# The first eight modulation slabs: from a sum on VectorE to products on TensorE

## The chip, the cores and the metric

One core of a Trainium2 chip runs the kernel. The metric is the device time of one execution in microseconds (us). Before the change the median of 3 runs is 2600.26 us (2599.4 to 2601.9).

## The reference, cut to what matters

The model is two blocks in a row on 256 tokens of width 2048. The work around the change is the very beginning of the first block:

```python
cond = jax.nn.silu(c)                       # (1, 2048)
mod = cond @ ada_w[i] + ada_b[i]            # ada_w[i]: (2048, 6144)
shift, scale, gate = jnp.split(mod, 3, axis=-1)
h = rms_norm(x, pre_g[i]) * (1 + scale[:, None, :]) + shift[:, None, :]
y = sgu_mixer(h, sgu_w_in[j], ...)          # begins with h @ w_in, w_in: (2048, 12288)
```

Everything is float32. The large products are made from rounded parts: a value is split into a high part (float32r) and the rest, and three products (high by high, rest by high, high by rest) are added.

## The kernel before, in words

All weights stream from HBM through a ring `raw` of four slabs of 1 MB (`RAWS = 4`; a slab is four tiles of 128 rows by 512 columns). SyncE's queue issues the loads in the order in which they are used (`load`, L291). Before each it waits for `raw_free`, which starts at four and which VectorE raises by one each time it has finished with a slab (`raw_done`, L1022 to L1027). The landing of slab n is told by the semaphore `landed[n % 4]`.

The first eight slabs of the ring (`ADA_HEAD = 8`) belong to `ada_w[0]`: four for the first 512 columns (the shift of model columns 0 to 511) and four for columns 2048 to 2559 (the scale of the same model columns). After them come the slabs of `sgu_w_in`, mixed with further slabs of `ada_w[0]`.

How `cond @ ada_w` is made before: the weight tile has the contracted rows on the partitions. VectorE multiplies each 128x512 tile by one column of `cond` (one number for each partition) and adds it to a running sum, in two chains (`ada_sum`, L1037; L1051 is the first product of a chain, L1047 a product with addition, L1056 adds the two chains). A slab costs four such instructions. When four slabs are summed, TensorE adds over the partitions (`pe_ada`, L1946): four matmuls with 128 columns of the sum as the stationary operand and a column of ones as the moving one, so each has one moving column. VectorE copies the four resulting columns out of PSUM (`ada_keep`, L1060).

The start, engine by engine:

- ScalarE loads `x` by DMA, waits for the small vectors, makes `cond` by Silu (L613), squares the two tiles of `x` for the norm (L535), takes the root (L542), scales both tiles to `y` (L619), and copies the eight groups of turned tiles out of PSUM into `xt` (L622).
- TensorE turns the small vectors (L2068, L2069), then the two tiles of `y` in eight groups of four 128x128 transposes (L2077), two PSUM banks in turn, then makes the two column sums (L1952).
- VectorE makes the eight slabs' sums with the steps of the norm in between, and then the shift and scale of the first four column tiles (`modulated`, L1258 to L1260, which tells `scales`).
- Then ScalarE writes the modulated tiles `tf` (L631, four instructions, one for each column tile) and their rounded part `a_hi` (L558, two), VectorE the rest `a_lo` (L1268, two), and the first product with `w_in` begins on TensorE (`pe_block`, `pe_chunk`, L1927 and L1932).

From there the work is in four phases of twelve blocks. Each phase covers four of the sixteen contracted column tiles, each block two chunks. For each chunk ScalarE rounds half a slab (`hi_next`, L437) and VectorE makes the rest (`lo_next`, L1018), three chunks ahead of TensorE (`AHEAD = 3`). The eight other slabs of `ada_w[0]` in each phase are summed by VectorE in the same way as the first eight.

Of the kernel before, what the change touches and what calls it, by code (L numbers as in the profile page):

```python
# [22 lines left out]
P = 128  # L23
T = 2
# [139 lines left out]
def build(nc, d, out):  # L164
    ctx = ExitStack()
    with ctx:
# [3 lines left out]
        def sem(name):  # L170
            return ctx.enter_context(nc.semaphore(name))
# [109 lines left out]
        lb_diff, lb_exp, h_gn, h_kf = (sem(k) for k in ("lb_diff", "lb_exp", "h_gn", "h_kf"))  # L281
        wt_zero, h_a_zero = sem("wt_zero"), sem("h_a_zero")
        lb_ready = sem("lb_ready")

# [7 lines left out]
        def load(sp, n, *parts):  # L292

            k = n.raw.base % RAWS
            sp.wait_ge(raw_free, n.raw.at(1))
            for place, source, adds in parts:
                sp.dma_start(place(raw[:, k, :]), source).then_inc(landed[k], adds)
            n.raw.base += 1
# [309 lines left out]
        def _(act):  # L608
            n = Counts()
            for t in range(T):  # L610
                act.dma_start(x[:, t, :], d["x"][0, t * P:(t + 1) * P, :]).then_inc(x_landed, 16)
            act.wait_ge(vec_kept, 1)
            nc.scalar.activation(cond[:, :], va[:, A_C:A_C + KT], ACT.Silu).then_inc(cond_ready, 1)  # L613
            act.wait_ge(x_landed, 32)
            act_squares(act, n, lambda t: x[:, t, :])
            act_root(act, n)
            act.wait_ge(n_rstd, n.nrm.base)
            for t in range(T):
                nc.scalar.activation(y[:, t, :], x[:, t, :], ACT.Copy, scale=rstd[:, t:t + 1]).then_inc(n_out, 1)  # L619
            for g in range(8):  # L620
                act.wait_ge(t_turned, g + 1)
                nc.scalar.activation(xt[:, 2 * g:2 * g + 2, :], ps[:, 3 + g % 2, :].rearrange("p (k s) -> p k s", k=2), ACT.Copy).then_inc(xt_kept, 1)  # L622

            def modulated(p):

                act.wait_ge(scales, p + 1)
                if p:
                    act.wait_ge(t_lo, 2 * p)
                for g in range(2 * p, 2 * p + 2):
                    for k in range(2 * g, 2 * g + 2):  # L630
                        ins = nc.scalar.activation(tf[:, g % 2, k % 2 * S:(k % 2 + 1) * S], xt[:, k, :], ACT.Identity,  # L631
                                                   bias=mod[:, 0, k:k + 1], scale=hscale[:, k:k + 1])
                    ins.then_inc(t_kept, 1)
                act_split(act, n, 2, a_hi[:, 4 * p:4 * p + 4, :], modulated=True, fresh=True)

# [424 lines left out]
        def ada_keep(dve, n, layer, col, bank=7, at=0):  # L1060

            dve.wait_ge(ada_summed, n.ada.at(1))
            nc.vector.tensor_copy(mod[:, layer, bass.ds(col, 4)], ps[:, bank, at:at + 4]).then_inc(ada_kept, 1)
            n.ada.base += 1
# [167 lines left out]
        def _(dve):  # L1232
# [3 lines left out]
            nc.vector.tensor_copy(vb[:, :], ps[:, 4, P:P + B_ROWS]).then_inc(vec_kept, 1)  # L1236
            dve.wait_ge(cond_ready, 1)
            early = (ps[:, 6, :], ps[:, 5, :])
            ada_sum(dve, n, 0, acc, early)
            n.sq.base += 2  # L1240
            dve.wait_ge(n_ss, n.sq.base)
            nc.vector.tensor_scalar(var[:, :], ss[:, :], 1.0 / D, EPS, ALU.mult, ALU.add).then_inc(n_var, 1)
            ada_sum(dve, n, 1, acc, early)
            dve.wait_ge(n_sd, n.nrm.base + 1)
            nc.vector.reciprocal(rstd[:, :], sd[:, :]).then_inc(n_rstd, 1)
            n.nrm.base += 1
            ada_sum(dve, n, 2, acc, early)
            ada_sum(dve, n, 3, acc, early)
            for a in range(3):
                ada_sum(dve, n, a, acc_s, early)  # L1250
            ada_keep(dve, n, 0, 0)
            ada_sum(dve, n, 3, acc_s, early)

# [24 lines left out]
            def phase_sum(m):  # L1278

                j = m % PHASE_W  # L1280
                if m < FIRST and j < PHASE_A:
                    ada_sum(dve, n, j % 4, (acc, acc_s)[j // 4], early)

            lo_next(dve, n, 0)
            ada_keep(dve, n, 0, 16)
            modulated(0)
            split(0)
# [659 lines left out]
        def pe_ada(pe, n, acc=acc, bank=7, at=0):  # L1947

            pe.wait_ge(ada_acc, n.ada.at(1))
            pe.wait_ge(ada_kept, n.ada.at(1))  # L1950
# [112 lines left out]
        def _(pe):  # L2063
# [6 lines left out]
            pe.wait_ge(vec_kept, 2)  # L2070
            pe.wait_ge(n_out, 2)
            for g in range(8):
                if g >= 2:
                    pe.wait_ge(xt_kept, g - 1)
                for k in range(2 * g, 2 * g + 2):
                    for t in range(T):
                        ins = nc.tensor.transpose(ps[:, 3 + g % 2, k % 2 * S + t * P:k % 2 * S + (t + 1) * P], y[:, t, k * P:(k + 1) * P], ident)  # L2077
                ins.then_inc(t_turned, 1)
            pe_ada(pe, n)
            pe_ada(pe, n, acc_s)  # L2080
            pe.wait_ge(xt_kept, 8)
            for p in range(PHASES):
                n.tg.base += 2
                n.kept.base += 2
                pe.wait_ge(t_lo, n.tg.base)
                for j in range(PHASE_W):
                    pe_block(pe, n, A, kts=4, k0=4 * p)
                    if j in (3, 7):
# [413 lines left out]
```

## Time and profile before

| What | Value |
| --- | --- |
| median of 3 runs | 2600.26 us |
| the profiled execution | 2598.19 us |
| its span (first to last instruction) | 2596.4 us |
| TensorE matmul busy | 2523.9 us, 97% |
| VectorE busy | 1631.5 us, 63% |
| ScalarE busy | 1361.4 us, 52% |
| mean DMA rate | 211 GB/s |
| mean granted TensorE clock | 0.991 |

The profile is of one execution. In its rows PE is TensorE's matmuls, PEld its loads of the stationary operand (they run beside matmuls), DVE VectorE, ACT ScalarE, POOL GpSimd, SP SyncE; a `q` behind a name is the engine's queue of DMA issues. `L1047` is line 1047 of the kernel. `a <- b` names the tile written and those read. Times are in us from the span's start, unless a row says ns. In square brackets stands the idle time of the engine ahead of a row and what ended it. PEclk is the granted clock of TensorE as a share of full speed: 1.00 is 2.4 GHz, 0.50 is 1.2 GHz.

### The profile page before, as it was taken

The page shows a single profiled execution, that of the slowest core. Times are in us where ns is not written, and L with a number is a line of the kernel's source. Part 1 is how long each engine was busy: PE and PEld are TensorE (multiplying, and loading weights), DVE is VectorE, ACT ScalarE, POOL GpSimd, SP SyncE. Part 2 cuts the span into 40 slices and gives each one's busy share as a digit, 9 for nine tenths or more (in the row PEclk, how much of TensorE's full clock was granted, in tenths as well). Part 3 has the DMA queues.
Part 4 walks back from the last instruction along what each step waited for, and adds up shares of the span by engine and source line. Part 5 has one row for each costly group of instructions (what it writes and reads, how often), then busy time and mean ns, then how long its engine had stood idle before and what let it go on. Part 6 is the DMA issues. An engine that isn't in the chain of part 4 may idle for free.

```text
span 2596.4 us, 33485 instructions
## 1 busy us (share of the span) xinstructions
PE 2523.9 (97%) x11958; PEld 2086.4 (80%) x11958; DVE 1631.5 (63%) x2512; ACT 1361.4 (52%) x1922; POOL 412.6 (16%) x288
## 2 busy tenths in 40 slices
PE   4999999999997999998999999999999999999999
PEld 3788788888886888887887787888888888888887
DVE  7779987767666677766655554555555545545544
ACT  4555764444446555555466666654544444444443
POOL 0155563111020000010000000034100011110111
PEclk8999999999998999999999999999999999999999
DMA  9889877877773776654645555545555555555554
GB/s 347 319 272 345 297 248 259 276 279 274 253 278 130 225 213 199 208 175 135 193 147 176 157 159 155 172 169 182 191 191 183 194 193 181 194 194 179 182 191 146
DMA packets 363831, 549.06 MB, mean 211 GB/s; under 512 B 32332, under 2 KB 126128, under 8 KB 363312
## 3 DMA queue, kind: packets, MB, share of 16 engines
q1 hardware_dynamic: 361872, 541.24, 63.0%
q10 hardware_dynamic: 1824, 6.04, 0.6%
q8 instruction: 83, 1.36, 0.2%
q14 instruction: 52, 0.43, 0.0%
HBM read 545.13 MB, written 2.10 MB: 211 GB/s over the span
## 4 chain that ended last, share of the span: by engine, by line
PE 92%; DVE 3%; issue 3%; ACT 2%; DMA 0%; SPq 0%; POOL 0%; ACTq 0%; DVEq 0%; POOLq 0%
PE ps L1927 54%; PE ps L1932 27%; PE ps L1912 1%; PE ps L1914 1%; PE ps L1913 1%; DVE ps L1047 1%; PE ps L2003 1%; PE ps L2234 1%; PE ps L1952 1%; DVE lo L1018 1%; ACT hi L437 1%; PE ps L2107 1%; PE ps L2233 1%; ACT tf L597 0%; PE ps L1989 0%
## 5 line engine op out<-in xcount | busy, mean ns | idle before, releaser
L1018 DVE TENSOR_TENSOR lo<-raw,hi 128x1024 fp32r<-128x1024 f32 x838 | 1081.5, 1302 | 749.6 <-ACT hi L437 748.7
L437 ACT ACTIVATE hi<-raw 128x1024 fp32r<-128x1024 f32 x838 | 881.6, 1060 | 759.8 <-PE ps L1932 658.9
L1927 PE MATMUL ps<-hi,a_hi 128*128 128x512 f32 (+1 forms) x2144 | 852.0, 397 | 6.9 <-issue 4.7
L1927 PE MATMUL ps<-hi,a_lo 128*128 128x512 f32 (+1 forms) x2144 | 837.3, 391 | 0.0
L1932 PE MATMUL ps<-lo,a_hi 128*128 128x512 f32 (+1 forms) x2144 | 574.1, 390 | 0.4 <-DVE lo L1018 0.4
L1927 PEld LDWEIGHTS ps<-hi,a_hi 128*128 128x128 f32 x2144 | 404.0, 188 | 95.4 <-issue 11.6
L1932 PEld LDWEIGHTS ps<-lo,a_hi 128*128 128x128 f32 x2144 | 402.9, 188 | 85.5 <-DVE lo L1018 1.0
L1927 PEld LDWEIGHTS ps<-hi,a_lo 128*128 128x128 f32 x2144 | 404.0, 188 | 79.3
L1927 PE MATMUL ps<-hi,b_hi 128*128 128x512 f32 x1024 | 404.1, 395 | 0.3 <-ACT y L766 0.3
L1927 PE MATMUL ps<-hi,b_lo 128*128 128x512 f32 x1024 | 399.4, 390 | 0.0
L1932 PE MATMUL ps<-lo,b_hi 128*128 128x512 f32 x1024 | 274.3, 390 | 0.0
L1932 PEld LDWEIGHTS ps<-lo,b_hi 128*128 128x128 f32 x1024 | 192.2, 188 | 40.9
L1927 PEld LDWEIGHTS ps<-hi,b_hi 128*128 128x128 f32 x1024 | 192.4, 188 | 39.1 <-ACT y L766 0.5
L1927 PEld LDWEIGHTS ps<-hi,b_lo 128*128 128x128 f32 x1024 | 192.4, 188 | 38.7
L1787 POOL TENSOR_TENSOR v<-v,stage 128x512 f32<-128x512 f32 (+1 forms) x88 | 145.0, 1648 | 436.6 <-ACT stage L456 295.1
L1047 DVE SCALAR_TENSOR_TENSOR ps<-raw,cond,ps 128x512 f32<-128x512 f32 x200 | 141.3, 749 | 1.1 <-DMA raw<-in_ada_w 1.1
L456 ACT ACTIVATE stage<-ps 128x512 f32<-128x512 f32 x156 | 84.6, 595 | 90.4 <-PE ps L1932 90.4
L1787 POOL TENSOR_TENSOR x<-x,stage 128x512 f32 (+1 forms) x38 | 65.5, 1722 | 355.2 <-ACT stage L456 351.9
L1787 POOL TENSOR_TENSOR v<-stage 128x512 f32 x32 | 34.2, 1069 | 323.0 <-ACT stage L456 319.8
L1787 POOL TENSOR_TENSOR v<-v 128x512 f32<-128x512 f32 x16 | 29.0, 1834 | 330.3 <-ACT v L466 330.0
L1787 POOL TENSOR_TENSOR y<-y,stage 128x512 f32<-128x512 f32 x30 | 50.9, 1696 | 168.5 <-ACT stage L456 166.3
L1047 DVE SCALAR_TENSOR_TENSOR acc_b<-raw,cond,acc_b 128x512 f32<-128x512 f32 x84 | 66.9, 797 | 0.0
(289 smaller groups left out, 1912.0 us busy)
## 6 DMA issues: line engine op xcount, KB each, us to landing
raw<-in_ada_w SPq DMA_DIRECT2D x96, 1024.0 KB
raw<-in_sgu_w_in SPq DMA_DIRECT2D x96, 1024.0 KB
raw<-in_w_up SPq DMA_DIRECT2D x64, 1024.0 KB
raw<-in_w_down SPq DMA_DIRECT2D x64, 1024.0 KB
raw<-in_w_in SPq DMA_DIRECT2D x42, 1024.0 KB
raw<-in_sgu_w_out SPq DMA_DIRECT2D x32, 1024.0 KB
raw<-in_w_in SPq DMA_DIRECT2D x128, 256.0 KB
raw<-in_mla_w_in SPq DMA_DIRECT2D x33, 512.0 KB
```

The lines of the kernel that those rows point to most:

```text
L437: nc.scalar.activation(hi[:, q % CHUNKS, :], raw[:, r % RAWS, q % 2 * CW:(q % 2 + 1) * CW], ACT.Copy).then_inc(hi_ready, 1)
L456: nc.scalar.activation(to, ps[:, 2 * s + t, 0:width], func, scale=rstd[:, t:t + 1] if normed else 1.0).then_inc(acc_free, 1)
L1018: nc.vector.tensor_tensor(lo[:, q % CHUNKS, :], raw[:, r % RAWS, q % 2 * CW:(q % 2 + 1) * CW], hi[:, q % CHUNKS, :].bitcast(F32), ALU.subt ...
L1047: ins = nc.vector.scalar_tensor_tensor(out=out[:, :] if a == j == 3 else to, in0=w, scalar=c, in1=to, op0=ALU.mult, op1=ALU.add)
L1787: return nc.gpsimd.tensor_tensor(out_, a, b, op)
L1912: mm(out_, w_hi, x_hi, start=start, stop=False)
L1913: mm(out_, w_hi, x_lo, start=False, stop=False)
L1914: return mm(out_, w_lo, x_hi, start=False, stop=stop)
L1927: nc.tensor.matmul(ps[:, 2 * s + t, 0:width], x[:, k0 + j, t * P:(t + 1) * P], hi[:, c, w], start=begins, stop=False)
L1932: ins = nc.tensor.matmul(ps[:, 2 * s + t, 0:width], x2[0][:, k0 + j, t * P:(t + 1) * P], lo[:, c, w], start=False, stop=last and j == kts - 1)
L1952: ins = nc.tensor.matmul(ps[:, bank, at + q:at + q + 1], acc[:, q * P:(q + 1) * P], ones[:, :], start=True, stop=True)
L2003: ins = nc.tensor.transpose(ps[:, 4 + n.tg.base % 2, e2 * S + t * P:e2 * S + (t + 1) * P], src(t, 2 * g + e2), ident)
```

## The change

- TensorE now makes the first eight slabs' products itself. `slab_product(a)` waits for slab a and makes sixteen matmuls: each has a 128x128 piece of the slab as the stationary operand and one column of `cond` as the moving one. The sixteen pieces of the contraction are added in PSUM, banks 4 to 7. VectorE's eight `ada_sum` calls and TensorE's two `pe_ada` calls at the start go.
- The loads of ring slabs 4 to 11 wait for `slab_used`, which TensorE raises after each product, and not for `raw_free`. VectorE adds eight to `raw_free` at once when all products are done, for the loads after them.
- Products and transposes of `x` are interleaved in TensorE's order: slabs 0 and 1, three groups of transposes, slab 2, three groups, slab 3, two groups, slab 4, slabs 5, 6 and 7.
- ScalarE squares `x` before it waits for the small vectors and makes `cond` (before: after it).
- The second tile of `y` is scaled by VectorE, and every second group of turned tiles is copied by VectorE (`xt_vec`).
- One VectorE copy takes all eight columns (shift and scale) out of PSUM. It stands ahead of the first `lo_next`.
- Of the first four modulated column tiles, ScalarE makes two and VectorE two (`tf_vec`), and TensorE's first chunk of each phase waits only for the first of the two groups of `a_lo`; it waits for the second after that chunk.

```diff
         def load(sp, n, *parts):
             k = n.raw.base % RAWS
-            sp.wait_ge(raw_free, n.raw.at(1))
+            if n.raw.turn is None and RAWS <= n.raw.base < ADA_HEAD + RAWS:
+                sp.wait_ge(slab_used, n.raw.base - RAWS + 1)
+            else:
+                sp.wait_ge(raw_free, n.raw.at(1))
...
+            act.wait_ge(x_landed, 32)
+            act_squares(act, n, lambda t: x[:, t, :])
             act.wait_ge(vec_kept, 1)
             nc.scalar.activation(cond[:, :], va[:, A_C:A_C + KT], ACT.Silu).then_inc(cond_ready, 1)
-            act.wait_ge(x_landed, 32)
-            act_squares(act, n, lambda t: x[:, t, :])
             act_root(act, n)
             act.wait_ge(n_rstd, n.nrm.base)
-            for t in range(T):
-                nc.scalar.activation(y[:, t, :], x[:, t, :], ACT.Copy, scale=rstd[:, t:t + 1]).then_inc(n_out, 1)
-            for g in range(8):
+            nc.scalar.activation(y[:, 0, :], x[:, 0, :], ACT.Copy, scale=rstd[:, 0:1]).then_inc(n_out, 1)
+            for g in range(0, 8, 2):
                 act.wait_ge(t_turned, g + 1)
-                nc.scalar.activation(xt[:, 2 * g:2 * g + 2, :], ps[:, 3 + g % 2, :].rearrange("p (k s) -> p k s", k=2), ACT.Copy).then_inc(xt_kept, 1)
+                nc.scalar.activation(xt[:, 2 * g:2 * g + 2, :], ps[:, 0, :].rearrange("p (k s) -> p k s", k=2), ACT.Copy).then_inc(xt_kept, 1)
...
-                for g in range(2 * p, 2 * p + 2):
+                for g in range(2 * p, 2 * p + 2 if p else 1):
...
+                if p == 0:
+                    act_split(act, n, 1, a_hi[:, 0:2, :], modulated=True, fresh=True)
+                    act.wait_ge(tf_vec, 1)
+                    act_split(act, n, 1, a_hi[:, 2:4, :], modulated=True, fresh=True)
+                else:
+                    act_split(act, n, 2, a_hi[:, 4 * p:4 * p + 4, :], modulated=True, fresh=True)
...
-            dve.wait_ge(cond_ready, 1)
             early = (ps[:, 6, :], ps[:, 5, :])
-            ada_sum(dve, n, 0, acc, early)
...
-            ada_sum(dve, n, 1, acc, early)
...
-            ada_sum(dve, n, 2, acc, early)
-            ada_sum(dve, n, 3, acc, early)
-            for a in range(3):
-                ada_sum(dve, n, a, acc_s, early)
-            ada_keep(dve, n, 0, 0)
-            ada_sum(dve, n, 3, acc_s, early)
+            dve.wait_ge(n_rstd, n.nrm.base)
+            nc.vector.tensor_scalar(y[:, 1, :], x[:, 1, :], rstd[:, 1:2], None, ALU.mult).then_inc(n_out, 1)
+            for g in range(1, 8, 2):
+                dve.wait_ge(t_turned, g + 1)
+                nc.vector.tensor_copy(xt[:, 2 * g:2 * g + 2, :], ps[:, 1, :].rearrange("p (k s) -> p k s", k=2)).then_inc(xt_vec, 1)
+            dve.wait_ge(slab_used, ADA_HEAD)
+            nc.vector.tensor_copy(mod[:, 0, 0:32].rearrange("p (c k) -> p c k", c=2)[:, :, 0:4],
+                                  ps[:, 4:8, 0:2].rearrange("p q c -> p c q")).then_inc(ada_kept, 2)
+            n.ada.base += 2
+            nc.vector.memset(tick[:, 0:1], 0.0).then_inc(raw_free, ADA_HEAD)
+            n.raw.base += ADA_HEAD
...
+            modulated(0)
+            dve.wait_ge(scales, 1)
+            dve.wait_ge(xt_vec, 4)
+            for k in range(2, 4):
+                ins = nc.vector.tensor_scalar(tf[:, 1, k % 2 * S:(k % 2 + 1) * S], xt[:, k, :], hscale[:, k:k + 1], mod[:, 0, k:k + 1], ALU.mult, ALU.add)
+            ins.then_inc(tf_vec, 1)
             lo_next(dve, n, 0)
-            ada_keep(dve, n, 0, 16)
-            modulated(0)
             split(0)
...
             pe.wait_ge(vec_kept, 2)
-            pe.wait_ge(n_out, 2)
-            for g in range(8):
+            pe.wait_ge(cond_ready, 1)
+
+            def slab_product(a):
+                pe.wait_ge(landed[a % RAWS], LAND * (a // RAWS + 1))
+                for r in range(4):
+                    for q in range(4):
+                        k = 4 * (a % 4) + r
+                        ins = mm(ps[:, 4 + q, a // 4:a // 4 + 1], raw[:, a % RAWS, r * NB + q * P:r * NB + (q + 1) * P], cond[:, k:k + 1],
+                                 start=k == 0, stop=k == KT - 1)
+                ins.then_inc(slab_used, 1)
+
+            def x_turned(g):
                 if g >= 2:
-                    pe.wait_ge(xt_kept, g - 1)
+                    pe.wait_ge(xt_vec if g % 2 else xt_kept, g // 2)
                 for k in range(2 * g, 2 * g + 2):
                     for t in range(T):
-                        ins = nc.tensor.transpose(ps[:, 3 + g % 2, ...], y[:, t, k * P:(k + 1) * P], ident)
+                        ins = nc.tensor.transpose(ps[:, g % 2, ...], y[:, t, k * P:(k + 1) * P], ident)
                 ins.then_inc(t_turned, 1)
-            pe_ada(pe, n)
-            pe_ada(pe, n, acc_s)
-            pe.wait_ge(xt_kept, 8)
+
+            slab_product(0)
+            slab_product(1)
+            pe.wait_ge(n_out, 2)
+            for a, groups in ((2, (0, 1, 2)), (3, (3, 4, 5)), (4, (6, 7))):
+                for g in groups:
+                    x_turned(g)
+                slab_product(a)
+            for a in range(5, ADA_HEAD):
+                slab_product(a)
+            n.ada.base += 2
+            pe.wait_ge(xt_kept, 4)
+            pe.wait_ge(xt_vec, 4)
             for p in range(PHASES):
                 n.tg.base += 2
                 n.kept.base += 2
-                pe.wait_ge(t_lo, n.tg.base)
+                pe.wait_ge(t_lo, n.tg.base - 1)
                 for j in range(PHASE_W):
-                    pe_block(pe, n, A, kts=4, k0=4 * p)
+                    pe_block(pe, n, A, kts=4, k0=4 * p, extra=None if j else {0: lambda: pe.wait_ge(t_lo, n.tg.base)})
```

## Rows read from the trace of the kernel before

**Rows 1.** The page: busy time, and the chain that ended last by engine.

```profile
PE 2523.9 (97%) x11958; PEld 2086.4 (80%) x11958; DVE 1631.5 (63%) x2512; ACT 1361.4 (52%) x1922; POOL 412.6 (16%) x288
...
PE 92%; DVE 3%; issue 3%; ACT 2%; DMA 0%; SPq 0%; POOL 0%; ACTq 0%; DVEq 0%; POOLq 0%
```

**Rows 2.** Stretches: window, us, busy of each engine, PEclk, DMA share, GB/s.

```profile
core 0: us, PE busy (x) PEld busy (x) DVE busy (x) ACT busy (x) POOL busy (x), PEclk, DMA share, GB/s
...
27.90:31.30 3.40, 2.56 (x21) 2.17 (x20) 3.40 (x8) 2.18 (x4) 0.00 (x0) 1.00 1.05 404
31.40:43.40 12.00, 1.86 (x8) 1.78 (x8) 8.39 (x19) 5.01 (x8) 0.00 (x0) 0.50 0.83 307
43.40:48.40 5.00, 4.92 (x12) 3.90 (x13) 4.85 (x8) 2.01 (x3) 0.00 (x0) 0.50 0.48 149
48.40:117.00 68.60, 68.60 (x312) 57.00 (x311) 55.02 (x89) 39.91 (x56) 0.00 (x0) 1.00 0.93 334
```

**Rows 3.** Timeline of the start: start, us, engine, line, operation.

```profile
11.47 0.40 PE L2069 MATMUL ps<-cst,tf 116*128 116x116 f32 x1
...
12.22 0.22 ACT L613 ACTIVATE cond<-va 128x16 f32<-128x16 f32 x1 [9.28 <-DVE va L1235]
...
12.94 1.41 DVE L1051 TENSOR_SCALAR ps<-raw,cond 128x512 f32<-128x512 f32 x2 [0.57 <-DMA raw<-in_ada_w]
...
16.39 1.28 ACT L542 ACT_TABLE_LOAD   x1
...
19.33 3.90 ACT L619 ACTIVATE y<-x,rstd 128x2048 f32<-128x2048 f32 x2 [1.44 <-DVE rstd L1245]
...
23.37 5.16 PE L2077 MATMUL ps<-cst,y 128*128 128x128 f32 x24 [11.50 <-ACT y L619]
...
33.35 1.06 ACT L437 ACTIVATE hi<-raw 128x1024 fp32r<-128x1024 f32 x1 [2.81 <-DMA raw<-in_sgu_w_in]
...
36.88 1.86 PE L1952 MATMUL ps<-ones,acc_s 128*128 128x1 f32 x8 [6.19 <-DVE acc_s L1056]
38.78 0.16 DVE L1063 COPY mod<-ps 128x4 f32<-128x4 f32 x1 [0.81 <-PE ps L1952]
...
39.45 2.08 ACT L631 ACTIVATE tf<-gain,mod,hscale 128x256 f32<-128x256 f32 x4 [5.04 <-DVE hscale L1260]
41.43 1.13 ACT L558 ACTIVATE a_hi<-tf 128x512 fp32r<-128x512 f32 x2
42.08 1.29 DVE L1268 TENSOR_TENSOR a_lo<-tf,a_hi 128x512 fp32r<-128x512 f32 x2 [2.67 <-ACT a_hi L558]
...
43.48 0.77 PE L1927 MATMUL ps<-hi,a_hi 128*128 128x512 f32 x1 [4.74 <-issue]
```

**Rows 4.** The transposes of line 2077, from 23.2 and from 28.7.

```profile
L2077 PE MATMUL ps<-cst,y x8: 421/421/448, 23.4 to 24.9; 128*128 128x128 f32 x8
...
L2077 PE MATMUL ps<-cst,y x7: 272/273/328, 28.8 to 29.5; 128*128 128x128 f32 x7
```

**Rows 5.** The critical chain (start, us): a column sum, a later chunk's first products.

```profile
67.84 0.79 PE ps L1952 x8
...
79.68 1.81 PE ps L1927 x8
```

**Rows 6.** Stretches around a column sum after a pause (columns as in rows 2).

```profile
789.00:790.70 1.70, 1.63 (x8) 1.66 (x8) 1.70 (x2) 0.00 (x0) 0.00 (x0) 0.50 1.15 361
790.70:795.50 4.80, 4.80 (x12) 3.83 (x13) 0.99 (x5) 0.00 (x0) 0.00 (x0) 0.50 0.98 375
795.50:796.00 0.50, 0.50 (x2) 0.34 (x2) 0.00 (x0) 0.00 (x0) 0.00 (x0) 0.51 1.05 410
```

**Rows 7.** Stretches around transposes and matmuls after a pause (same columns).

```profile
127.00:130.00 3.00, 2.87 (x9) 2.48 (x10) 3.00 (x6) 0.00 (x0) 2.62 (x2) 0.50 0.82 278
130.00:131.00 1.00, 1.00 (x5) 0.77 (x5) 1.00 (x2) 0.00 (x0) 0.00 (x0) 0.80 1.06 358
```

**Rows 8.** Groups by line: mean ns of one instruction ahead of the idle time.

```profile
L1205 DVE TENSOR_SCALAR y<-x,rstd 128x512 f32<-128x512 f32 x16 | 7.2, 482 | 0.1
L1018 DVE TENSOR_TENSOR lo<-raw,hi 128x1024 fp32r<-128x1024 f32 x8 | 9.7, 1223 | 1.0 <-ACT hi L437 1.0
```

**Rows 9.** Timeline, the rounding that comes latest against TensorE in the first phase.

```profile
76.40 1.06 ACT L437 ACTIVATE hi<-raw 128x1024 fp32r<-128x1024 f32 x1 [4.86 <-DMA raw<-in_sgu_w_in]
```

More of the change, by code:

```diff
@@ L282, in build @@
         wt_zero, h_a_zero = sem("wt_zero"), sem("h_a_zero")
+        slab_used, xt_vec, tf_vec = sem("slab_used"), sem("xt_vec"), sem("tf_vec")
         lb_ready = sem("lb_ready")
@@ L628, in modulated @@
                     act.wait_ge(t_lo, 2 * p)
-                for g in range(2 * p, 2 * p + 2):
+                    act.wait_ge(xt_vec, 4)
+                for g in range(2 * p, 2 * p + 2 if p else 1):
                     for k in range(2 * g, 2 * g + 2):
@@ L632, in modulated @@
                                                    bias=mod[:, 0, k:k + 1], scale=hscale[:, k:k + 1])
-                    ins.then_inc(t_kept, 1)
-                act_split(act, n, 2, a_hi[:, 4 * p:4 * p + 4, :], modulated=True, fresh=True)
+                    ins.then_inc(t_kept, 1 if p else 2)
+                if p == 0:
[4 more added lines that the diff above has]
+                    act_split(act, n, 2, a_hi[:, 4 * p:4 * p + 4, :], modulated=True, fresh=True)
             def scaled(k):
@@ L1060, in ada_keep @@
         def ada_keep(dve, n, layer, col, bank=7, at=0):
-            dve.wait_ge(ada_summed, n.ada.at(1))
+            dve.wait_ge(ada_summed, n.ada.at(-1))
             nc.vector.tensor_copy(mod[:, layer, bass.ds(col, 4)], ps[:, bank, at:at + 4]).then_inc(ada_kept, 1)
@@ L1947, in pe_ada @@
         def pe_ada(pe, n, acc=acc, bank=7, at=0):
-            pe.wait_ge(ada_acc, n.ada.at(1))
+            pe.wait_ge(ada_acc, n.ada.at(-1))
             pe.wait_ge(ada_kept, n.ada.at(1))
@@ L2070, in _ @@
             pe.wait_ge(vec_kept, 2)
-            pe.wait_ge(n_out, 2)
-            for g in range(8):
+            pe.wait_ge(cond_ready, 1)
[8 more added lines that the diff above has]
+            def x_turned(g):
                 if g >= 2:
-                    pe.wait_ge(xt_kept, g - 1)
+                    pe.wait_ge(xt_vec if g % 2 else xt_kept, g // 2)
                 for k in range(2 * g, 2 * g + 2):
                     for t in range(T):
-                        ins = nc.tensor.transpose(ps[:, 3 + g % 2, k % 2 * S + t * P:k % 2 * S + (t + 1) * P], y[:, t, k * P:(k + 1) * P], ident)
+                        ins = nc.tensor.transpose(ps[:, g % 2, k % 2 * S + t * P:k % 2 * S + (t + 1) * P], y[:, t, k * P:(k + 1) * P], ident)
                 ins.then_inc(t_turned, 1)
-            pe_ada(pe, n)
-            pe_ada(pe, n, acc_s)
-            pe.wait_ge(xt_kept, 8)
+            slab_product(0)
[10 more added lines that the diff above has]
+            pe.wait_ge(xt_vec, 4)
             for p in range(PHASES):
```

## The prediction

> **What bounds the kernel now.** I read the page first: TensorE is busy for 97% of the span and makes 92% of the chain that ended last [rows 1]. So a change of the start can only pay by letting TensorE's long run begin sooner, and what it delays there comes back in full. Next I cut the start into stretches: TensorE does almost nothing until 43.4, then it is busy without a gap to 117 [rows 2]. The figure of merit is thus one instant, the start of the first product with `w_in`, T = 43.48 [rows 3]. The timeline shows what holds it: VectorE sums slabs from 12.94 on, the last column sum ends at 38.74 (36.88 + 1.86), and then come the copy, the scales, `tf`, `a_hi` and `a_lo` [rows 3]. That tail is 43.48 - 38.74 = 4.74 us.
>
> DMA is a second floor. The first slab of `w_in` lands at 33.35 [rows 3], at a rate of 404 GB/s [rows 2], behind the eight slabs of `ada_w`: (33.35 - 12.94) / 8 = 2.55 us a slab. No order of the other engines beats it.
>
> **The clock, read from durations.** The clock column says 1.00 from the start to 31.3, but the transposes contradict it: 421 ns each from 23.4, 273 ns from 28.8 [rows 4]. So TensorE was at 1.2 GHz when the transposes began and came to 2.4 GHz during them, near 28. It fell again near 31.4, after the last transposes and eight one-column matmuls [rows 2, 3], and was low until 48.4. This matters because the new products are one-column matmuls. Their price is known at both clocks: 8 in 0.79 us at the high one [rows 5], 8 in 1.86 us at the low one [rows 3]. Less the last one's own length (about 0.35 of the 1.86), the low pace is (1.86 - 0.35) / 7 = 0.214 us; the high one is 0.79 / 8 = 0.099.
>
> Which clock will they have? The best witness is at 789: the engine comes out of a pause at the low clock, makes eight one-column matmuls without a gap (1.63 us busy in 1.70), then 512-column matmuls without a gap, and the clock rises only near 796, 7 us after it began [rows 6]. After the pause at 127 it began with four transposes and went on with 512-column matmuls, and the clock was up within 3.4 us [rows 7]. No row shows a rise behind one-column matmuls alone, and a fall stands behind them at 31.4. I take the low clock.
>
> **Part by part.**
> 1. Products on TensorE. They begin when `cond` (12.44) and slab 0 (12.94) are there [rows 3]. One slab is 16 x 0.214 = 3.42 us at the low clock, eight are 27.4. At the high clock they are 16 x 0.099 = 1.58 and 12.7: these are the two bounds.
> 2. Transposes, 32 as before, now between the products: 5.16 / 24 = 0.215 us each [rows 3], 6.9 in all. Two of each three groups have their bank free; waiting for the copy of the group two before costs me 0.3 in all (between 0 and the 2.7 or so that a single copier would make of it; two copiers make it the low end).
> 3. Sum: 12.94 + 27.4 + 6.9 + 0.3 + 0.1 for the end of the last = 47.6 for the last product, where 38.74 stood.
> 4. The waits that are added. SyncE's loads of slabs 4 to 11 stand behind TensorE's products, and nothing else is queued behind them there. At the low clock slab 4's load goes out at about 16.4 and is used at about 34; slab 8, the first of `w_in`, goes out at about 37 and has landed by 42, well before 47.6. So DMA is off the path. `n_out` is wanted at 12.94 + 6.8 = 19.8. ScalarE's squares (two of about 2 us) move ahead of `cond` into the wait for the small vectors. The root then follows at about 12.5: table load 1.28, root 0.2, reciprocal 0.2, then `y` on two engines, ScalarE's 3.90 / 2 = 1.95 [rows 3] beside VectorE's 4 x 0.482 = 1.93 [rows 8], ready at 16.1. If the new order needs one more table load ahead of Silu, `cond` is late by 0.9 (bound: 0 to 1.3); I take 0, since at 12.94 the slab is the later of the two.
> 5. The sums that VectorE loses (32 instructions of 0.7 us, 12.94 to 36.8) were the path before and are gone; what is late next is TensorE.
> 6. The tail. Copy and scales as before: 39.45 - 38.74 = 0.71, so `scales` at 48.3. ScalarE makes two `tf` instead of four: 2.08 / 2 = 1.04, then `a_hi` 0.57: 49.9. VectorE makes the other two: no row shows 128x256 from SBUF; between 0.24 each (half of 0.482) and 0.5 each, I take 0.3 (nearer the row of 482 ns): 48.9. Then its `lo_next` of 1.22 [rows 8], which before was done ahead of the column sum and now stands in the path: 50.1 to 50.2. Then one `a_lo` of 0.65 (1.29 / 2) where two were waited for: 50.9. TensorE starts at T = 51.0. The tail is 3.4 us, shorter than 4.74 by 1.3.
> 7. The rest. The split wait in later phases saves at most one `a_lo`, 0.65 us, and there TensorE has no gap to fill before 117 [rows 2]: 0. VectorE's next steps (second `a_lo`, then `lo_next`) end 0.5 later against T than before; TensorE's first chunk takes over 5 us at the low clock, which hides it.
> 8. The low clock after T costs the same as before: it was low for 5.0 us after 43.4 [rows 2], which is 2.5 us lost. With another start against the clock it may be 1.7 to 3.4.
>
> T moves by 51.0 - 43.5 = +7.5. The later work is paced by TensorE and its own ring, so it moves with T. The profiled execution takes 2598.19 us (span 2596.4 and 1.8 around it): 2605.7. The median of the runs shown is 2.07 above that execution, and so is my forecast for the median: 2600.26 + 7.5 = 2607.8.
>
> **The Trainium skill against this.** "TensorE: Matmul & The Clock Gate", "What's actually happening", says that the clock depends on how busy the engine has been lately and that activity releases the throttle. A reader would call sixteen back-to-back matmuls busy, which gives rival A. The rows at 789 speak against it, the rise near 28 for activity in general. The same page, "PE-mode transpose", says that transposes do not bring the full clock; the rows at 23.4 and 28.8 show it coming up during transposes alone, so here the measurement decides, and it leaves rival B its chance.
>
> **Rivals.**
> A. The products bring the clock up (faster). Product 0 and part of 1 are slow, then each is 1.58 and each transpose 0.14 or so. TensorE keeps up with DMA: slab 7 lands at 33.35 - 2.55 = 30.8, the last product ends at 32.5 to 33. `scales` is at 33.7, but ScalarE's first `hi` waits for `w_in` until 33.35 and ends at 34.4. `tf` 35.4, `a_hi` 36.0, `a_lo` 36.7: T = 36.9, -6.6 us, 2593.7. For: the general statement above, and that PE was not always at work near 31.4. Against: rows 6. It decides if the clock is up before product 3. 20%.
> B. The low clock holds for the products, but a batch of three groups of transposes (2.6 us) lifts it for one stretch, as near 28. A stretch of 3.4 us at the high clock, as in rows 2 from 27.9, does the work of about 7: T is 3.4 sooner, +4.1, 2604.4; with parts of it 2602 to 2605. 13%.
> C. As A, but the gain is given back: ScalarE's `hi` at 76.40 waits for DMA and ends at 77.46, TensorE wants it at 79.68 [rows 5, 9], a slack of 2.2 us. DMA after the first slabs is refilled relative to VectorE, which moves with T, so little of it should be lost: about 2.4 to 4 of 6.6, 2597 to 2598. 4%.
> D. The products do not overlap their weight loads: each costs its whole length, 0.352 by the row at 36.88 (1.86 less seven paces). Then a slab takes 5.6 us, T is later by another 8 x 2.2 = 17.7, 2625. In the rows at 36.88 they do overlap. 5%.
> My forecast: 58%.
>
> **How the numbers follow.** A run of three tells 0.2%, 5.2 us, from no change; slower is above 2605.5, faster below 2595.1. Slower: forecast 0.58 (a little of it falls under the bound), D 0.05, less that little: 0.60. Faster: A, nearly all, with a little for what I have not thought of: 0.22. Same: B, C and the edge: 0.18. The forecast's own range is 2605 to 2611 (0.9 for `cond`, 1.7 to 3.4 for the clock after T, 0.5 in the tail, 0.6 in the copies' waits, 1 of the runs). To hold 8 in 10 it has to take in B and most of A: 2593 to 2611.
>
> **What would show it.** Durations of the new matmuls: 352 ns and a pace of 0.21 us (right), 250 and 0.10 (rival A). Last product's end at 47.6, copy right behind it, first L1927 at about 51. Slab loads 4 to 7 going out 3.4 us apart or more. Squares ending before `cond`, `y` ready near 16, TensorE reaching the first transpose after 19. The clock column low in most of 13 to 51. I am wrong if the clock column is 1.00 and the durations agree with it before the fourth product.

## The result: 1.3% slower, four times the loss that was forecast

The changed kernel takes 2632.1 us (median of 4 runs, 2628.67 to 2636.45) against 2599.83 for the kernel before (4 runs): ratio 1.0127, 95% interval 1.0114 to 1.0139. Timed again beside the kernel before on another occasion it took 2632.63 against 2599.17, ratio 1.0130 (1.0114 to 1.0145). The forecast was 2607.8, range 2593 to 2611: right in its sign, 24.3 us too low, and outside the range by 21.1. The changed kernel's profiled execution takes 2628.67 us, the fastest of its four; its span is 2626.9, and all its rows are from that one. Of all the executions timed here three were slow (4723.59, 7501.12 and 13706.63 us), and no time or ratio below uses them.

The shares on the profile's page show nothing of a loss, which is a lesson in itself: TensorE is even busier.

```profile
PE 2571.5 (98%) x12198; PEld 2134.8 (81%) x12198; DVE 1611.1 (61%) x2477; ACT 1356.2 (52%) x1916; POOL 412.5 (16%) x288
```

Against [rows 1] TensorE's busy time has grown by 47.6 us and VectorE's has fallen by 20.4. What tells is the timeline of the start (start, us, engine, line, operation), as in [rows 3]:

```profile
9.13 1.91 ACT L539 ACTIVATE stage<-x 128x2048 bf16<-128x2048 f32 x1 [6.18 <-DMA x<-in_x]
...
13.18 1.28 ACT L619 ACT_TABLE_LOAD   x1
...
14.47 0.22 ACT L619 ACTIVATE cond<-va 128x16 f32<-128x16 f32 x1
14.71 1.28 ACT L546 ACT_TABLE_LOAD   x1
...
14.79 13.78 PE L2094 MATMUL ps<-cond,raw 128*128 128x1 f32 x64 [2.71 <-ACT cond L619]
...
28.44 2.90 PE L2104 MATMUL ps<-cst,y 128*128 128x128 f32 x12
...
31.13 3.77 PE L2094 MATMUL ps<-cond,raw 128*128 128x1 f32 x32
...
34.76 2.95 PE L2104 MATMUL ps<-cst,y 128*128 128x128 f32 x12
...
37.50 3.98 PE L2094 MATMUL ps<-cond,raw 128*128 128x1 f32 x32
...
41.35 1.68 PE L2104 MATMUL ps<-cst,y 128*128 128x128 f32 x8
...
55.70 14.43 PE L2094 MATMUL ps<-cond,raw 128*128 128x1 f32 x67
...
70.24 0.17 DVE L1259 COPY mod<-ps 128x8 f32<-128x8 f32 x1 [26.48 <-PE ps L2094]
...
70.91 1.09 ACT L635 ACTIVATE tf<-gain,mod,hscale 128x256 f32<-128x256 f32 x2 [13.73 <-DVE hscale L1271]
70.91 0.73 DVE L1299 TENSOR_SCALAR tf<-gain,hscale,mod 128x256 f32<-128x256 f32 x2
71.56 1.22 DVE L1027 TENSOR_TENSOR lo<-raw,hi 128x1024 fp32r<-128x1024 f32 x1
72.03 1.15 ACT L562 ACTIVATE a_hi<-tf 128x512 fp32r<-128x512 f32 x2
72.69 1.29 DVE L1279 TENSOR_TENSOR a_lo<-tf,a_hi 128x512 fp32r<-128x512 f32 x2
...
73.60 0.77 PE L1942 MATMUL ps<-hi,a_hi 128*128 128x512 f32 x1 [3.47 <-issue]
```

The reader is to see three things. The first two slabs take 64 rows and 13.65 us (14.79 to 28.44), so one slab is 32 rows, where the program has sixteen matmuls. Slabs 2 and 3 take 3.63 and 3.85 us to the start of the next row group, the first two 6.83 each. In the text a row of such a product is called a pass; what the engine does inside one the trace cannot tell. And the first product with `w_in` begins at 73.60, where it was 43.48 [rows 3]: 30.12 us later, of 30.5 us that the span grew (2626.9 - 2596.4). The whole loss is ahead of that instant; the rest took 2552.9 us before and 2553.3 after.

The clock over the same stretches (columns as in [rows 2]):

```profile
14.80:28.40 13.60, 13.60 (x64) 13.60 (x65) 1.46 (x2) 3.40 (x3) 0.00 (x0) 1.00 0.64 233
31.20:34.60 3.40, 3.40 (x32) 3.40 (x31) 0.00 (x0) 0.60 (x1) 0.00 (x0) 1.00 0.56 214
34.60:37.40 2.80, 2.80 (x15) 2.47 (x15) 0.69 (x1) 0.60 (x1) 0.00 (x0) 0.54 0.46 105
37.50:41.30 3.80, 3.80 (x33) 3.80 (x33) 0.69 (x1) 0.00 (x0) 0.00 (x0) 0.90 0.48 188
42.80:70.10 27.30, 27.30 (x130) 27.24 (x128) 0.69 (x1) 1.07 (x2) 0.00 (x0) 0.50 0.46 153
```

In the first row the column says 1.00, but the durations of the products there say otherwise (again as in [rows 4]): their median is 352 ns from 14.8 to 28.2, as long as at the recorded low clock later, and 250 in slab 2.

```profile
L2094 PE MATMUL ps<-cond,raw x64: 344/352/352, 14.8 to 28.2; 128*128 128x1 f32 x64
```

```profile
L2094 PE MATMUL ps<-cond,raw x30: 213/250/348, 31.1 to 34.4; 128*128 128x1 f32 x30
```

So the column is of no use ahead of the first change that the profile records; from there on it and the durations agree. The first row shows one thing more: PEld is busy for all of its 13.60 us, so the weight loads follow each other without a gap, at 0.21 us each. The DMA share of 0.46 to 0.64, where it was full before (1.05 in the first row of [rows 2]), tells that the slabs now wait for TensorE.

### The profile page after: what moved, and what is told of

Read it like the earlier page. It is cut to its first block, busy times and chain, and to the rows that moved or that the text cites. A ratio compares the mean times of both kernels' runs of the same rounds, so it can differ in the third digit from the quotient of the medians.

```text
span 2626.9 us, 33920 instructions
## 1 busy us (share of the span) xinstructions
PE 2571.5 (98%) x12198; PEld 2134.8 (81%) x12198; DVE 1611.1 (61%) x2477; ACT 1356.2 (52%) x1916; POOL 412.5 (16%) x288
## 4 chain that ended last, share of the span: by engine, by line
PE 93%; DVE 3%; issue 2%; ACT 2%; DMA 1%; ACTq 0%; DVEq 0%
PE ps L1942 53%; PE ps L1947 26%; PE ps L2094 2%; PE ps L1927 1%; PE ps L1929 1%; PE ps L1928 1%; PE ps L2018 1%; PE ps L2271 1%; DVE lo L1027 1%; PE ps L1967 1%; PE ps L2270 1%; ACT hi L441 1%; PE ps L2144 1%; DVE ps L1056 0%; ACT tf L601 0%
## 5 line engine op out<-in xcount | busy, mean ns | idle before, releaser
L1056 DVE SCALAR_TENSOR_TENSOR ps<-raw,cond,ps 128x512 f32<-128x512 f32 x174 | 123.8, 748 | 1.3 <-DMA raw<-in_ada_w 1.3
```

The source lines that it names most:

```text
L1056: ins = nc.vector.scalar_tensor_tensor(out=out[:, :] if a == j == 3 else to, in0=w, scalar=c, in1=to, op0=ALU.mult, op1=ALU.add)
```

## The experiments

Each run is beside the kernel before on the same chip, and a ratio is to that. T is the start of the first product with `w_in` in the profile. Three theories stood at the outset. P: the price is the number of passes (of weight loads), two for each float32 matmul, and the low clock doubles it. R: the products wait for slabs. C: something is paid for each matmul whatever its type; the bfloat16 run tells it from P.

### Half of the matmuls

```diff
-                for r in range(4):
+                for r in (0, 3):
```

> The changed kernel with half of the matmuls of each of the eight slab products (two of the four row tiles of each slab; the other half of the contraction is left out of the sum). Theory P, the price is the number of weight loads: each float32 matmul is two passes in the trace (256 records for 128 matmuls), each pass 0.214 us at the low clock, so half of them saves about 27 us of the 55: first product with w_in near 46 to 50 instead of 73.6, time 2604 to 2609. Rival R, the slabs come late or are freed late (the ring), and the products wait: the pace of the products stays near 6.8 us a slab, time above 2620.

Measured: 2605.8 us (10 runs), ratio 1.0024 (1.0014 to 1.0034); T = 49.14.

```profile
14.56 6.96 PE L2094 MATMUL ps<-cond,raw 128*128 128x1 f32 x32 [2.46 <-ACT cond L619]
...
24.07 3.41 PE L2094 MATMUL ps<-cond,raw 128*128 128x1 f32 x16
...
30.13 1.93 PE L2094 MATMUL ps<-cond,raw 128*128 128x1 f32 x16
...
32.83 12.84 PE L2094 MATMUL ps<-cond,raw 128*128 128x1 f32 x64
```

Sixteen rows and 3.41 us a slab at the low clock: this is the price that the forecast had put on the whole product. R falls: nothing waits between the groups. C does not fall by this run, because half of the matmuls are half of either price. The first batch of transposes, at 21.4, was not followed by a faster slab here (3.41 us from 24.07), the second was (1.93 us from 30.13).

### All transposes behind the products

```diff
-            slab_product(0)
-            slab_product(1)
-            pe.wait_ge(n_out, 2)
-            for a, groups in ((2, (0, 1, 2)), (3, (3, 4, 5)), (4, (6, 7))):
-                for g in groups:
-                    x_turned(g)
-                slab_product(a)
-            for a in range(5, ADA_HEAD):
-                slab_product(a)
+            for a in range(ADA_HEAD):
+                slab_product(a)
+            pe.wait_ge(n_out, 2)
+            for g in range(8):
+                x_turned(g)
```

> The changed kernel with all eight slab products first and all transposes behind them. Clock theory: the transposes between the products lifted the clock for a stretch each time, so that slabs 2 and 3 took 3.8 and 4.0 us and not 6.85. Without them all eight products run at the low clock, 8 x 6.85 = 55 us, and the time is 5 to 7 us longer than the changed kernel's profiled 2628.7: 2634 to 2637. Rival: slabs 2 and 3 were faster for another reason (their data lay ready), then they are as fast here and the time is 2628 to 2632.

Measured: 2636.17 us (3 runs), ratio 1.0144 (1.0123 to 1.0164); T = 79.54, 5.9 later than in the changed kernel.

```profile
14.63 54.75 PE L2094 MATMUL ps<-cond,raw 128*128 128x1 f32 x256 [2.72 <-ACT cond L619]
69.23 3.43 PE L2104 MATMUL ps<-cst,y 128*128 128x128 f32 x16
72.82 2.72 PE L2104 MATMUL ps<-cst,y 128*128 128x128 f32 x16 [0.16 <-ACT gain L625]
79.54 0.77 PE L1942 MATMUL ps<-hi,a_hi 128*128 128x512 f32 x1 [3.99 <-issue]
```

```profile
L2094 PE MATMUL ps<-cond,raw x256: 344/352/353, 14.6 to 69.0; 128*128 128x1 f32 x128
```

The second fence is the line's group (ns min, median, max): one unbroken run of 256 passes stays at the low clock's length for 54.75 us, at a pace of 0.2135 us. So these one-column matmuls did not bring the clock up in 54.75 us, and in the changed kernel, where the only difference is the order, it came up behind transposes, twice. The rival falls too: slabs 2 and 3 are slow here although their data lay ready. "TensorE: Matmul & The Clock Gate" of the Trainium skill says ("What's actually happening") that busy-ness releases the throttle. An engine busy in every row for 55 us did not release it here; the measurement decides. The same page's section "PE-mode transpose" has it that transposes do not bring the full clock. Here too the measurement decides against it: before the change the transposes went from 421 to 273 ns with nothing but transposes on the engine [rows 4].

### Wide matmuls between the products

```diff
                                  start=k == 0, stop=k == KT - 1)
+                    if r % 2:
+                        mm(ps[:, 2, :], ident, cst[:, 0:NB], start=True, stop=True)
```

> The changed kernel with two float32 matmuls of 512 columns put into each slab product, whose result nobody reads. Clock theory: matmuls with many columns between the one-column ones keep the clock up; a slab then takes 3.8 + 2 x 0.86 = 5.5 us instead of 6.85 although there is more to do: a few us faster than the changed kernel, 2622 to 2630, with the clock column at 1.00 from about 20 on. Rival, the clock is not moved by them: each slab takes 6.85 + 3.4, the time is about 27 us longer, near 2659.

Measured: 2654.47 us (3 runs), ratio 1.0207 (1.0186 to 1.0227). My expectation failed; the rival's held, 4.5 us under its 2659. T = 103.10.

```profile
17.96 2.05 PE L2097 MATMUL ps<-cst 128*128 128x512 f32 x2
19.81 3.41 PE L2094 MATMUL ps<-cond,raw 128*128 128x1 f32 x16
23.08 2.05 PE L2097 MATMUL ps<-cst 128*128 128x512 f32 x2
24.93 3.41 PE L2094 MATMUL ps<-cond,raw 128*128 128x1 f32 x16
```

The pattern repeats to 99.5 with one short rise near 50, behind transposes (at 50.41 a half slab takes 1.7 us). Each half slab has 1.8 us of wide matmul and 3.3 us of one-column ones, and with this mix the clock stayed low. This filler was paid at the low clock too, so it did not buy the high one; other mixes were not run.

### The operands swapped

```diff
-                    for q in range(4):
-                        k = 4 * (a % 4) + r
-                        ins = mm(ps[:, 4 + q, a // 4:a // 4 + 1], raw[:, a % RAWS, r * NB + q * P:r * NB + (q + 1) * P], cond[:, k:k + 1],
-                                 start=k == 0, stop=k == KT - 1)
+                    k = 4 * (a % 4) + r
+                    ins = mm(ps[0:1, 4 + a // 4, :], cond[:, k:k + 1], raw[:, a % RAWS, r * NB:(r + 1) * NB], start=k == 0, stop=k == KT - 1)
...
+            pe.wait_ge(ada_acc, 1)
+            for c in range(2):
+                for q in range(4):
+                    ins = mm(ps[:, 7, 4 * c + q:4 * c + q + 1], (acc, acc_s)[c][0:1, q * P:(q + 1) * P], ones[0:1, :], start=True, stop=True)
+            ins.then_inc(ada_summed, 1)
```

> The changed kernel with the operands of the slab products swapped, still float32: the condition's column is stationary and the slab's 512 columns move, so a slab is four matmuls with 512 columns and the result is a row, which VectorE copies and eight small matmuls turn into columns. Weight-load theory with the clock: the columns cost 4 x 1.71 = 6.8 us a slab at the low clock and 3.4 at the high one, and these matmuls, unlike the one-column ones, bring the clock up. First product with w_in near 55 to 60 instead of 73.6: 2612 to 2618. Rival, the clock stays low as with the fillers: about 76, 2632 to 2636.

Measured: 2613.3 us, ratio 1.0052 (1.0036 to 1.0068); T = 56.56, both as expected.

```profile
14.56 9.36 PE L2097 MATMUL ps<-raw,cond 128*1 128x512 f32 x16 [2.65 <-ACT cond L619]
...
25.79 3.59 PE L2097 MATMUL ps<-raw,cond 128*1 128x512 f32 x8
...
35.89 13.89 PE L2097 MATMUL ps<-raw,cond 128*1 128x512 f32 x32
```

Here the clock comes up and stays: 3.47 us a slab in the last group (13.89 / 4). It is the better form of this product, 17 us ahead of the changed kernel in T, and still behind VectorE: the last product ends at 49.8, where the column sum ended at 38.74 [rows 3]. A slab of TensorE's at the high clock (3.47 here, 3.63 to 3.85 above) costs more than VectorE's sum of one: 12.94 to 36.8 for eight, 3.0 each, with the steps of the norm among them. The row form pays at its end too: T follows the last product by 6.8 us, where it was 3.5 in the changed kernel, for the copies and small matmuls that turn the row.

### The products in bfloat16

The upper 16 bits of each slab value and of the condition are multiplied, so this computes the first modulation columns more coarsely than the others.

```diff
-raw[:, a % RAWS, r * NB + q * P:r * NB + (q + 1) * P], cond[:, k:k + 1],
+raw[:, a % RAWS, r * NB + q * P:r * NB + (q + 1) * P].bitcast(BF16)[:, 1::2], cond[:, k:k + 1].bitcast(BF16)[:, 1:2],
```

> The changed kernel with the slab products in bfloat16 (the upper halves of slab and condition, so the products are only coarse). Theory P: one pass and one weight load for each matmul, 128 records instead of 256, and 27 us less or more than that if a bfloat16 weight load is also shorter: 2604 or less, down to DMA's floor near 2595. Rival C, the pace of small matmuls is set by something that is paid for each matmul whatever its type (issue, PSUM, reading the slab): as the records are halved but each takes twice as long, the time stays near 2632.

Measured: 2593.69 us (10 runs), ratio 0.9981 (0.9972 to 0.9991): faster than both kernels, and 1.3 us under the 2595 that I had called DMA's floor. T = 38.24.

```profile
14.63 0.57 PE L2094 MATMUL ps<-cond,raw 128*128 128x1 bf16 x16 [2.79 <-ACT cond L619]
...
29.63 0.58 PE L2094 MATMUL ps<-cond,raw 128*128 128x1 bf16 x16 [3.08 <-DMA raw<-in_ada_w]
32.11 0.59 PE L2094 MATMUL ps<-cond,raw 128*128 128x1 bf16 x16 [1.90 <-DMA raw<-in_ada_w]
...
34.60 1.06 ACT L441 ACTIVATE hi<-raw 128x1024 fp32r<-128x1024 f32 x1 [8.76 <-DMA raw<-in_sgu_w_in]
```

The loads of the stationary operand, in this run and in the changed kernel (ns min, median, max):

```profile
L2094 PEld LDWEIGHTS ps<-cond,raw x128: 96/104/152, 14.6 to 32.5; 128*128 128x128 bf16 x128
```

```profile
L2094 PEld LDWEIGHTS ps<-cond,raw x64: 288/333/333, 14.8 to 28.2; 128*128 128x128 f32 x64
```

Sixteen rows for a slab, one for each matmul, and a pace of 0.58 / 16 = 0.036 us where a float32 matmul took 2 x 0.2135 = 0.427. Both are at the low clock: the column reads 0.50 from 28 to 33 in this run. That is a twelfth: not only the second pass goes, each load is shorter. C falls with that, and P as well if it counts passes alone, for a row has no fixed price. TensorE now waits for the last two slabs, and behind them ScalarE waits until 34.60 for the first slab of `w_in`, which holds the tail: DMA is the bound. "TensorE: Matmul & The Clock Gate" of the Trainium skill, "Weight-path perf modes", says that the faster way of loading weights is chosen for 128 weights of a type that is not float32; the trace agrees as far as it goes, 104 ns a load against 333. "FP8 and Floating Point Precision" of the Trainium skill, "TensorE Precision Notes", puts a true float32 product at four passes. The trace shows two rows for each, and cannot tell what is inside a row.

### The tail, reordered

```diff
-            hi_next(act, n, 0)
             modulated(0)
+            hi_next(act, n, 0)
...
-            lo_next(dve, n, 0)
             split(0)
+            lo_next(dve, n, 0)
```

> The bfloat16 kernel with one more step: ScalarE modulates and rounds the first column tiles before it rounds the first slab of w_in, and VectorE makes a_lo before its first lo. In the bfloat16 kernel the last product ended at 32.7, but ScalarE waited for the slab of w_in to 34.6 and only then made tf. Theory: DMA's landing and not TensorE bounds it, and the order lets the tail run beside the landing: first product at 36.1 instead of 38.2, 2 us less, 2591.5 where the bfloat16 kernel has 2593.7. Rival: the next wait (the first lo, the second slab's landing) takes it back, no change.

Measured: 2593.84 us (10 runs), ratio 0.9980 (0.9970 to 0.9989). T came to 36.60 where 36.1 was expected, 1.64 earlier than in the bfloat16 kernel, but the time did not follow: this version had 0.9980, that one 0.9981. The rival's time held, but not by the waits that it named: T did move. In the profiles the clock is low for longer behind T. In this version a 512-column matmul has its short length of 0.39 to 0.40 from 42.6 on, 6.0 us after T:

```profile
42.28 0.47 PE L1942 MATMUL ps<-hi,a_lo 128*128 128x512 f32 x1
...
42.59 0.40 PE L1942 MATMUL ps<-hi,a_hi 128*128 128x512 f32 x1
```

In the bfloat16 kernel four of them take 1.07 us (1.91 at the low clock) at 41.5 already, 3.2 us after its T:

```profile
41.48 1.08 PE L1947 MATMUL ps<-lo,a_hi 128*128 128x512 f32 x4
```

The difference of 2.7 us at half speed costs about 1.4 (an estimate), nearly all of the 1.64. Whether that is so in every execution, or the gain is lost in the spread of the runs (2590.48 to 2596.26), is not settled.

### Silu ahead of the squares again

```diff
-            act.wait_ge(x_landed, 32)
-            act_squares(act, n, lambda t: x[:, t, :])
             act.wait_ge(vec_kept, 1)
             nc.scalar.activation(cond[:, :], va[:, A_C:A_C + KT], ACT.Silu).then_inc(cond_ready, 1)
+            act.wait_ge(x_landed, 32)
+            act_squares(act, n, lambda t: x[:, t, :])
```

> The changed kernel with Silu ahead of the squares again, as before the change. Table theory: squares first costs one more table load (1.28 us) ahead of Silu and puts the condition behind the squares, so the products began at 14.8 and not at 12.9. Here they begin at 12.9 and everything is 1.9 us earlier: about 2 us under the changed kernel, if the stretches at the high clock fall alike. Rival: the products would have waited anyhow (for x to be normal, before slab 2), then no change.

Measured: 2631.26 us (4 runs, 2630.47 to 2635.19), ratio 1.0123 (1.0108 to 1.0139).

```profile
12.91 13.79 PE L2094 MATMUL ps<-cond,raw 128*128 128x1 f32 x64 [1.12 <-DMA raw<-in_ada_w]
...
35.62 6.83 PE L2094 MATMUL ps<-cond,raw 128*128 128x1 f32 x32
```

The products begin at 12.91, as the table theory has it. The time is not told apart from the changed kernel's, for the condition that I had put to it did not hold: in this execution slab 3 (the row at 35.62) ran at the low clock, 6.83 us and not 3.98, and T was 74.82, later than 73.60. The same transposes stood ahead of it, 1.6 us earlier than in the changed kernel. Whether it is this instant that decides is not shown: one profile at each is too few.

### The end of the change alone, and all but the products

The first is the kernel before with the shared modulation and the split wait (ScalarE's part is as in the change and left out here):

```diff
+            dve.wait_ge(scales, 1)
+            dve.wait_ge(xt_kept, 8)
+            for k in range(2, 4):
+                ins = nc.vector.tensor_scalar(tf[:, 1, k % 2 * S:(k % 2 + 1) * S], xt[:, k, :], hscale[:, k:k + 1], mod[:, 0, k:k + 1], ALU.mult, ALU.add)
+            ins.then_inc(tf_vec, 1)
             split(0)
...
-                pe.wait_ge(t_lo, n.tg.base)
+                pe.wait_ge(t_lo, n.tg.base - 1)
```

> The kernel before with only the end of the change: VectorE makes two of the four modulated tiles and TensorE waits only for the first group of a_lo. Theory: the tail is worth 1.3 to 1.6 us by itself (first product at about 41.9 instead of 43.5), so 2598.0 to 2598.5 where the kernel before has 2599.8. Rival: VectorE, the busy engine there, pays for its two tiles what ScalarE saves, 0.

Measured: 2598.15 us (11 runs), ratio 0.9994 (0.9985 to 1.0003); T = 42.10, 1.4 sooner. The profile agrees with the theory, the time cannot tell it from nothing.

The second is the change with VectorE's eight sums in place of the products; the loads wait for `raw_free` again, and the transposes and the two column sums stand in one row as before. Its main part:

```diff
-            dve.wait_ge(slab_used, ADA_HEAD)
+            ada_sum(dve, n, 0, acc, early)
+            for a, g in ((1, 1), (2, 3), (3, 5)):
+                ada_sum(dve, n, a, acc, early)
+                copied(g)
+            for a in range(3):
+                ada_sum(dve, n, a, acc_s, early)
+                if a == 0:
+                    copied(7)
```

> The change without the products: VectorE makes the eight slab sums as before, and all the rest of the change is in (squares first, shared norm, shared copies, shared modulation). Theory: the rest loads VectorE, which is then the path again: condition 2 us later, 1.3 for the second y, 2.8 for four copies, less 1.3 in the tail: first product at 48 to 50, time 2604 to 2607, so 25 us or more of the changed kernel's 32 are the products' alone. Rival: the rest is what costs (the ring waits, or the copies), and the time stays above 2620; or it pays, and the time is under 2598.

Measured: 2601.97 us (11 runs), ratio 1.0010 (1.0001 to 1.0019); T = 47.99 in the profile. The time is 2 us under the range that I had given, and T a hair under its own. The loss is 1.8 us in the median and 4.5 in T, and the two differ because the profiled execution, 2606.29 us, is among the slowest of the eleven. Of the changed kernel's loss the products, with the ring's new wait, then have some 30 of 32 us by the medians and 25.6 of 30.1 by T.

### The changed kernel once more

> The changed kernel itself once more, beside the kernel before on this chip, in more runs. If the stretches at the high clock behind the batches of transposes come in some executions and not in others, its times spread over some 8 us, 2628 to 2637, and its profile's first product lies between 73 and 80. If they always come, the times agree within 2 or 3 us.

Measured: 2628.4, 2633.08, 2633.25 and 2632.17; with the first four runs (2628.67, 2634.73, 2636.45, 2629.47) that is a spread of 8 us. Its profile has both lifts (slabs 2 and 3 in 3.72 and 3.94 us) and T = 73.33. The spread fits lifts that come in some executions and not in others, and the kernel without lifts lies at its upper end. But there is no profile of the slower executions, and the mean granted clock of each execution speaks only in part for it. A lift ends in a recorded fall, and the low stretch behind it pulls the mean down; without a recorded change ahead of T the column reads 1.00 there, and the kernel without lifts has 0.993 to 0.994. Of the eight executions two read so, 0.994 and 0.995, and took 2634.73 and 2633.25 us; they had no lift followed by a fall. The six others, at 0.984 to 0.987, lie between 2628.4 and 2636.45. By this reading the slowest of all had a lift too, and lifts are not the whole of the spread. It is so with Silu ahead of the squares as well: the profiled execution, with one lift, reads 0.985 and took 2635.19 us, the three others read 0.995 and took 2630.47 to 2631.72.

## Why the prediction was wrong, step by step

**Step 1, the products: the term that failed.** I read the row of eight at 36.88 [rows 3] as eight matmuls. The kernel's loop there has four (`for q in range(4)`). A float32 one-column matmul is two rows in the trace, and 0.214 us is the pace of a pass. A slab is 32 passes, 6.83 us, and eight are 54.75 with no lift, not 27.4. (The pace itself was right: (1.86 - 0.35) / 7 is 0.216 and not the 0.214 that stands there, and 0.2135 was measured.) I was misled by the transposes beside them: 32 in the program, 32 rows. What I called rival D, another cause for more than 3.42 us a slab, came nearest in size (5.6 us a slab, 2625 in all) and had the wrong mechanism: the loads do overlap. With the right count rival A would have had 8 x 3.2 = 25 us of products even at the high clock: 12.94 + 25 + 4.6 of transposes = 42.5, behind the 38.74 of the kernel before, so by this estimate it would not have gained either.

**The clock: mechanism right, with a part of rival B.** One-column matmuls did not raise it. Transposes did, behind the first two batches, for one slab each: 2 x 6.83 - 3.63 - 3.85 = 6.2 us were saved, and about as much in its second profile. The forecast gave rival B one such stretch and 3.4 us.

**Step 2**, transposes: 2.69 + 2.74 + 1.47 = 6.9 us with their waits; forecast 7.2.

**Step 4**, the condition: bounds 0 to 1.3, value taken 0, measured 1.85 (14.79 for 12.94). The order squares, Silu, root needs a table load that Silu, squares, root does not (13.18), and Silu also stands behind both squares. The ring and `n_out` were off the path as forecast.

**Step 6**, the tail: 73.60 - 70.13 = 3.47; forecast 3.4. VectorE's two tiles took 0.73, forecast 0.6.

**Steps 7 and 8**: behind T nothing changed, 2552.9 us before, 2553.3 after.

The sum: T was forecast 7.5 later and was 30.1 later. Of the difference of 22.6, the second pass makes +27.4, the lifts -6.2, the condition +1.85; transposes, pace and tail make up the -0.4 that is left. By the medians the loss is 32.3 us; the 2.2 us more than in T are not explained, and lie within the spread of the executions. The bounds of step 1 were drawn from the two clocks alone, both with the same wrong count, and so the range could not hold the result. The sign was right with the wrong count; the right count gives it more firmly.

## What to carry to other kernels

Before a duration is multiplied by a count, divide the rows of the trace by the instructions of the loop that made them; a float32 matmul here was two rows, a float32 transpose one. A matrix-vector product with the matrix stationary cost TensorE 0.43 us here for each 128x128 of float32 at the low clock (0.23 to 0.24 in the lifted slabs), and did not bring the clock up by itself; it lost to a VectorE sum of the same tiles, and in bfloat16 it won, down to the rate at which DMA brings the slabs. When one instant starts a long stretch that one engine paces (here TensorE), measure a change by that instant: in the twelve profiles here the rest took 2551 to 2557 us.

## What the runs showed of the hardware

- TensorE, busy without a gap for 54.75 us with one-column float32 matmuls, stayed at 1.2 GHz. With 1.8 us of 512-column matmuls after every 3.3 us it stayed there too, but for one short rise.
- Behind a batch of twelve 128x128 transposes, 2.7 us among such matmuls, the clock was high for about one slab in some cases (slabs 2 and 3 in both profiles of the changed kernel) and not in others (slab 3 with Silu first, slab 2 with half of the matmuls).
- The granted clock column reads 1.00 ahead of the first recorded change, whatever the clock: 352 ns a pass in that stretch is the low clock's duration.
- One-column matmuls with 128x128 stationary, both at the low clock: 0.427 us in float32, 0.036 us in bfloat16.
- With one column stationary and 512 float32 columns moving, the clock came up and a slab took 3.47 us, two rows for each matmul again.
- ScalarE loaded tables twice with Silu ahead of the squares and the root, and three times with the squares ahead of Silu, 1.28 us each.
